# A hybrid decoder block on one Trainium2 core: output projection and expert queries of two chunks from one filling of the weights, stages dealt anew, residual summed by TensorE

## The chip, the cores and the metric

One core of a Trainium2 chip. The metric is the time of one execution on the device in microseconds, the median of three runs. All data are float32.

## The reference

One decoder layer over 1024 tokens of width 1024, in chunks of 128 tokens. Cut to what matters:

```python
h = _rmsnorm(x, ln1_w)
proj = h @ w_in                       # 3592 columns, split for retention and gated DeltaNet
y_r = ...                             # retention, 4 heads, state carried from chunk to chunk
y_g = ...                             # gated delta rule, 4 heads, a triangular solve per chunk
x = x + concat([y_r, y_g]) @ w_out
h2 = _rmsnorm(x, ln2_w)
q = h2 @ peer_wq                      # 8 heads x 2 halves x 128
s = q . peer_keys                     # top 16 of 128 per half, top 16 of 256 sums
act = gelu(peer_u[ids] . h2)          # 128 experts for each token
x = x + sum(softmax(best) * act * peer_v[ids])
y = _rmsnorm(x, lnf_w)
```

Each token picks 128 experts, and each expert's rows of `peer_u` and `peer_v` are fetched by an indirect transfer: 8 KB for a token and expert, over 1 GB for the whole input.

## The kernel before

The sequence is eight chunks n = 0 to 7 of 128 tokens. The program is written by hand for each engine, with semaphores; nothing is scheduled automatically.

**Expert steps.** A chunk has 64 steps, 512 in all, numbered through. A step takes two gathers of 1 MB (`uv<-uv_tab,ids`, L459 on GpSimd) into a ring of ten buffers `uv`. VectorE forms the dot product of the u half with the token (L1209), ScalarE makes the gelu (L886) and two scaled diagonals (L892), TensorE multiplies the v halves by them into two PSUM banks, one pair of banks for each chunk (L488, eight instructions a step), and that frees the two ring buffers (`v_used`, for which GpSimd waits). TensorE works one step behind. After a chunk's last step, `add_sums` on VectorE (L1220) adds the banks to `acc` (the chunk's rows after the output projection), ScalarE squares and takes the root (L902, L904), VectorE scales (L1228), ScalarE issues the store. These run in steps 3 and 4 of the next chunk.

**Everything else is dealt between the steps.** Every engine walks the same list of stages and asks before each piece for the steps up to a place (`Stream`, `chunks`):

- *mix n*: convolution, retention, delta rule with the inversion of a triangular matrix in seven levels, then output projection (`out0`, `out1`), the residual sum, the transposes of the second norm and the queries of heads 0 to 3 (`q0`, `q1`, scores `s0`). Its pieces lie at places given by the weights `PIECES`, one `turn()` each.
- *route n*: the queries `q2`, `q3` and scores, the copies of the normalised row for the dot products (`replicate`), on VectorE the top 16 searches and the indices of the experts, and then the input projections of the next chunk or pair (`inputs`). Chunks 2+3, 4+5, 6+7 ("first", "second") share one filling of the input weights: each weight block is multiplied by both chunks' columns, `actT` and `actT_ahead`.

Where a stage lies is set by `window(n)`: the stages end at steps -3 (mix 0), 22, 55, 83, 118, 138, 176, 206, 244, 264, 304, 334, 372, 392, 436 and 456 (route 7). Route n must have found the experts of chunk n before step 64 n needs them.

**Weights.** The SP queue loads blocks of 1 MB: 14 for the inputs, 4 for the output projection, 8 for the queries. After the first ones they alternate between two buffers `wbuf`; a load waits for the last product that read its buffer. SP takes its list strictly in order, so a load that waits holds back all behind it. L540 (`rows_product`) and L548 (`cols_product`) are half projections, 16 or 32 instructions; `project` makes one for each source and half.

**Buffers.** `acc[n % 2]` takes the rows of chunk n and keeps the residual until the chunk is done; the load of chunk n waits until chunk n-2 is stored. `rowbuf` and `actT_ahead` (as `x_ahead`) also take the rows of the next chunks for the first norm. Products rotate through six PSUM banks in a queue (`take`).

## Time and profile before

| | |
|---|---|
| median of three runs | 3092.14 us (3088.72 to 3095.03) |
| span of the profiled execution | 3087.4 us |
| moved by DMA | 1265.78 MB, mean 410 GB/s |
| TensorE busy | 2363.0 us (77%), mean granted clock 0.879 |
| VectorE busy | 2096.2 us (68%) |
| ScalarE busy | 1174.9 us (38%) |
| GpSimd busy | 1164.5 us (38%) |

The span runs from the first instruction to the last one; it is the only time that the page gives of the profiled execution, and the median of the runs is 4.7 us above it. A busy share is a mean over stages that have different limits. Transfers are not an engine of the program: their busy share and rate stand in rows of their own. Line numbers are those of the kernel printed above.

### The profile page before, as it was taken

Reading aid. Unit: us, or ns where it says so; the run is one execution under the profiler, and the core shown is the slowest. Engines: PE = TensorE matmul, PEld = TensorE weight load, DVE = VectorE, ACT = ScalarE, POOL = GpSimd, SP = SyncE. Lnnn points to the kernel's source line nnn. Section 1 sums busy time; section 2 is a strip of 40 time slices with the busy share of each in tenths; the row PEclk is TensorE's granted clock in tenths of the full one; section 3 lists DMA queues with packets and bytes.
Section 4 is the critical chain, followed back from the end, with each engine's and each line's share of the span. In section 5 each row is a group of like instructions: output and inputs, shape, how many; then the busy total and the mean of one; then the engine's idle time right before and its main releaser. Section 6 shows DMA issues by size and latency. Waiting matters only on the chain.

```text
span 3087.4 us, 36329 instructions
## 1 busy us (share of the span) xinstructions
PE 2363.0 (77%) x12368; PEld 1353.8 (44%) x12368; DVE 2096.2 (68%) x5609; ACT 1174.9 (38%) x3433; POOL 1164.5 (38%) x1030
## 2 busy tenths in 40 slices
PE   8877787997875788897876688799787568866555
PEld 7753355763541345663452245575345124521111
DVE  5476955768579854767649974666856986497554
ACT  2243443344434432445323533434443443233222
POOL 0132533335433443324334443334433354335442
PEclk9999999999997899998997788899899788976777
DMA  8399999999999999999999999999999999999997
GB/s 354 139 410 426 427 427 411 414 403 416 426 426 404 426 427 426 417 418 426 427 426 415 424 426 427 417 404 419 427 426 426 413 427 427 427 407 425 427 427 333
DMA packets 177737, 1265.78 MB, mean 410 GB/s; under 512 B 21520, under 2 KB 21776, under 8 KB 25104
## 3 DMA queue, kind: packets, MB, share of 16 engines
q0 software_dynamic: 147456, 1073.81, 83.2%
q1 hardware_dynamic: 28368, 183.72, 14.3%
q10 hardware_dynamic: 1728, 5.94, 0.5%
q8 instruction: 98, 1.61, 0.2%
q14 instruction: 87, 0.71, 0.1%
HBM read 1259.19 MB, written 4.19 MB: 409 GB/s over the span
## 4 chain that ended last, share of the span: by engine, by line
PE 36%; DMA 30%; DVE 21%; ACT 7%; issue 4%; POOL 2%; ACTq 0%; POOLq 0%; DVEq 0%
DMA uv<-uv_tab,ids 25%; PE bank L488 13%; DVE uv L1209 10%; PE bank L548 9%; PE bank L540 8%; DMA wbuf<-w 5%; PE bank L555 2%; ACT diag L892 2%; POOL uv L459 2%; DVE area L1519 1%; DVE area L1274 1%; DVE area L1515 1%; PE bank L515 1%; PE bank L570 1%; DVE arena L1575 1%
## 5 line engine op out<-in xcount | busy, mean ns | idle before, releaser
L459 POOL DMA_INDIRECT uv<-uv_tab,ids x1024 | 1164.0, 1137 | 1890.0 <-PE bank L488 1542.2
L1209 DVE CUSTOM_DVE_ANT_0 uv<-uv,h 128x1024 f32<-128x1024 f32 x1024 | 1238.5, 1224 | 733.4 <-DMA uv<-uv_tab,ids 722.2
L488 PE MATMUL bank<-uv,diag 128*64 128x512 f32 x4096 | 1197.2, 717 | 532.3 <-ACT diag L892 528.8
L488 PEld LDWEIGHTS bank<-uv,diag 128*64 128x64 f32 x4096 | 288.9, 155 | 1205.5 <-ACT diag L892 751.5
L886 ACT ACTIVATE gelu<-dots 128x2 f32<-128x2 f32 x512 | 104.1, 203 | 1334.0 <-DVE dots L1209 1313.6
L548 PE MATMUL bank<-actT,wbuf 128*128 128x128 f32 x2688 | 338.8, 287 | 34.7 <-DMA wbuf<-w 29.8
L548 PEld LDWEIGHTS bank<-actT,wbuf 128*128 128x128 f32 x2688 | 326.4, 202 | 83.9 <-issue 67.5
L892 ACT ACTIVATE diag<-gated,gelu 128x64 f32<-128x64 f32 x1024 | 300.6, 340 | 59.9 <-ACT gelu L886 2.0
L882 ACT ACTIVATE gated<-smalls,gate 128x64 f32<-128x64 f32 x1024 | 294.3, 336 | 15.2 <-DVE acc L1228 15.2
L540 PE MATMUL bank<-wbuf,actT 128*128 128x256 f32 x960 | 227.1, 390 | 17.2 <-DMA wbuf<-w 15.3
L540 PEld LDWEIGHTS bank<-wbuf,actT 128*128 128x128 f32 x960 | 181.6, 194 | 89.1 <-issue 50.4
L555 PEld LDWEIGHTS bank<-arena 128*128 128x128 f32 x1016 | 127.9, 201 | 63.1 <-issue 45.9
L555 PE MATMUL bank<-arena 128*128 128x128 f32 x1016 | 141.7, 293 | 4.6 <-DVE arena L1418 2.4
L886 ACT ACT_TABLE_LOAD x92 | 118.0, 1283 | 1.6
L1519 DVE FIND_INDEX8 area<-area,arena 128x8 uint32<-128x128 f32 (+1 forms) x384 | 100.4, 280 | 0.0
L540 PE MATMUL bank<-wbuf,actT_ahead 128*128 128x256 f32 x384 | 88.7, 384 | 0.0
L1515 DVE MAX8 area<-arena 128x8 f32<-128x128 f32 (+1 forms) x384 | 81.8, 275 | 6.3 <-ACT arena L1126 4.6
L1209 DVE DVE_READ_ACCUMULATOR2_ANT dots<- 128x1 f32 x1024 | 84.2, 82 | 0.0
L1274 DVE SCALAR_TENSOR_TENSOR area<-conv_in,conv_w,area 128x128 f32<-128x128 f32 x288 | 82.1, 347 | 2.5
L540 PEld LDWEIGHTS bank<-wbuf,actT_ahead 128*128 128x128 f32 x384 | 71.5, 190 | 23.6 <-issue 14.6
L605 PE MATMUL bank<-keys_sb,arena 128*128 128x128 f32 x256 | 43.1, 318 | 44.5 <-ACT arena L914 42.8
L914 ACT ACTIVATE conv_in<-bank 128x512 f32<-128x512 f32 x24 | 14.3, 598 | 149.9 <-PE bank L548 149.8
(226 smaller groups left out, 1910.7 us busy)
## 6 DMA issues: line engine op xcount, KB each, us to landing
wbuf<-w SPq DMA_DIRECT2D x146, 1024.0 KB
uv<-w SPq DMA_DIRECT2D x20, 1024.0 KB, 18.1
uv<-uv_tab,ids POOLq DMA_INDIRECT x1024
acc<-x SPq DMA_DIRECT2D x8, 512.0 KB
y<-acc ACTq DMA_DIRECT2D x8, 512.0 KB
rowbuf<-x SPq DMA_DIRECT2D x5, 512.0 KB, 12.8
actT_ahead<-x SPq DMA_DIRECT2D x3, 512.0 KB, 18.8
keys_sb<-keysT ACTq DMA_DIRECT2D x1, 1024.0 KB, 12.9
```

Source lines behind the costliest of these rows:

```text
L459: nc.gpsimd.indirect_dma_start(out=uv[i % RING][:, :, :].rearrange("p z d -> p (z d)"), out_offset=None, in_=uv_tab, in_offset=bass.Indire ...
L488: done = mm(sums[s // PAIRS][z][64 * j:64 * j + 64, :], diag[:, i % DIAGS, :], uv[i % RING][:, 1, 512 * z:512 * z + 512], start=(s % PAIRS ...
L540: last = mm(b[:, WB * half_:WB * half_ + WB], src[:, k, :], wb[:, k, :], start=(k == 0), stop=(k == KT - 1))
L548: last = mm(b[:, o:o + P], wb[:, k, P * i:P * i + P], src[:, k, :], start=(k == 0), stop=(k == KT - 1))
L555: last = mm(b[:, P * h:P * h + P], lhs[:, h, :], rhs[:, h, :], start=True, stop=True)
L882: made = A(gated[:, step % 2, j, :], stack, ACT.Copy, scale=gate[n % 2][:, j, pair:pair + 1])
L886: A(gelu[:, step % 2, :], dots[:, d0:d0 + 2], ACT.Gelu).then_inc(S["gelu"], 1)
L892: made = A(diag[:, (2 * step + j) % DIAGS, :], gated[:, step % 2, j, :], ACT.Copy, scale=gelu[:, step % 2, j:j + 1])
L1209: V.tensor_tensor_reduce(out=u, in0=u, in1=h2[n % 2][:, j, :], scale=1.0, scalar=0.0, op0=ALU.mult, op1=ALU.add, accum_out=dots[:, i % DOT ...
L1274: last = V.scalar_tensor_tensor(dst, src, conv_w[:, i, j:j + 1], dst, ALU.mult, ALU.add)
L1515: last = V.max(vals(t)[:, o:o + 8], src(t))
L1519: last = V.max_index(index(t)[:, o:o + 8], vals(t)[:, o:o + 8], src(t))
```

## The change

**One filling for two chunks.** Chunks 4+5 and 6+7 (`JOINT`) make output projection and queries together. Mix 4 now ends after the mixed columns' transposes. Mix 5 makes its own, then multiplies each block of `w_out` and `peer_wq` by both chunks' columns (`out_and_first_queries`, `next_joint_queries`), with `actT` for chunk 4 and `actT_ahead` for chunk 5. Heads 4 to 7 follow in route 4, for both chunks; route 5 has only the search. The same for 6 and 7. The queries and scores of two chunks at once lie in `qT`, `scores`, `vnew` and `kst` (half of `rowbuf`).

**Stages dealt anew.** The new list `STAGES` gives each stage's end: -3, 22, 52, 76, 106, 124, 155, 178, 203 (mix 4), 244 (mix 5), 264 (route 4), 286 (route 5), 317 (mix 6), 372 (mix 7), 392 (route 6), 414 (route 7). In mix 5 and 7 `PIECES` sums to 47.9 for 37.9; in mix 4 and 6 to 27.1.

**Residual by TensorE.** At a chunk's first step TensorE multiplies `acc` by the identity into the two sum banks, which start from that; `add_sums` is gone, and ScalarE squares and VectorE scales straight from the banks, in halves. The output is staged in the other `acc`, so the load of chunk n waits for the store of chunk n-3.

**Waits.** The load of `x_ahead` for chunk 7 waits for `rep3` of chunk 5 (the last reader of `actT_ahead`, at step 264), the load of chunk 6's rows into `rowbuf` for the scores `s3` of chunk 5. TensorE may take a later bank of its queue where the first would be freed too late (`HELD`), and the sum banks of a finished chunk return to the queue at step 6.

```diff
+JOINT = (4, 5, 6, 7)
+TOGETHER = ("x2", "qT", "scores")
+def key(n):
+    return KIND[n] + "'" * (n in JOINT)
...
+        for j in range(2):
+            uses += both_chunks(f"out{j}", "x2", 2, j)
+        uses += [(f"h2T{j}-", "h2T", 2, j, -1) for j in range(2)] + h2T
+        for i in range(4):
+            uses += both_chunks(f"q{i}", "qT", 4, i) + both_chunks(f"s{i}", "scores", 4, i)
+        return uses + [(f"rep{i}-", "rep", 4, i, -1) for i in range(4)] + rep
...
-PIECES = ([2, 2.3, 1.7, 1, 1.6, 1.2, 2, 1.5]
-          + [1.2, 0.8, 0.7, 0.8, 1.3, 0.8, 1.2, 0.8, 0.7, 0.8, 0.5, 0.8] + [0.6, 0.8, 1.4, 0.6]
-          + [1.15, 1.15, 1.15, 1.15] + [0.8, 0.8] + [1.15, 1.15, 1.15, 1.15])
-WINDOW = {"first": (16, 14), "second": (12, 8), None: (12, 8)}
-def window(n):
-    if n < 0:
-        return -1, -1
-    if n < 3:
-        return ((-3, 22), (55, 83), (118, 138))[n]
-    before, after = WINDOW[KIND[n + 1] if n + 1 < NCH else None]
-    return PAIRS * n - before, PAIRS * n + after
+MIXED = ([2, 2.3, 1.7, 1, 1.6, 1.2, 2, 1.5]
+         + [1.2, 0.8, 0.7, 0.8, 1.3, 0.8, 1.2, 0.8, 0.7, 0.8, 0.5, 0.8] + [0.6, 0.8, 1.4, 0.6])
+PIECES = {key(n): MIXED + [1.15] * 4 + [0.8, 0.8] + [1.15] * 4 for n in range(NCH)}
+PIECES["first'"] = MIXED
+PIECES["second'"] = MIXED + [1.15] * 8 + [0.8, 0.8, 0.8] + [1.15] * 8
+STAGES = [("route", -1, -1), ("mix", 0, -3), ("route", 0, 22), ("mix", 1, 52), ("route", 1, 76), ("mix", 2, 106),
+          ("route", 2, 124), ("mix", 3, 155), ("route", 3, 178), ("mix", 4, 203), ("mix", 5, 244), ("route", 4, 264),
+          ("route", 5, 286), ("mix", 6, 317), ("mix", 7, 372), ("route", 6, 392), ("route", 7, 414)]
...
+        def queries(n, j):
+            if n not in JOINT:
+                return qT[:, 4 * j:4 * j + 4, :]
+            if j == 3:
+                return kst if later_of_two(n) else vnew
+            o = (12, 8, 12)[j]
+            return scores_of_chunk(n)[:, o:o + 4, :]
+        def scores_of_chunk(n):
+            return qT if later_of_two(n) else scores
...
                 if c.kind == "first":
+                    if n - 1 in JOINT:
+                        sp.wait_ge(full, PLACE[n - 1, "rep3"] + 1)
                     sp.dma_start(x_ahead, x[n + 1]).then_inc(ahead_loaded, 16)
                 if c.kind != "second":
                     weights(range(2 if n == 0 else 0, IN_BLOCKS))
-                if n >= 2:
-                    sp.wait_ge(y_stored, 16 * (n - 1))
-                sp.dma_start(acc[n % 2][:, :], x[n]).then_inc(x2_loaded, 16)
-                weights(range(IN_BLOCKS, BLOCKS))
+                if n == 2:
+                    sp.wait_ge(x2_taken, 1)
+                if n >= 3:
+                    sp.wait_ge(y_stored[(n - 3) % 2], 32 * ((n - 3) // 2 + 1))
+                sp.dma_start(acc[n % 2][:, :], x[n]).then_inc(x2_loaded[n % 2], 16)
+                if key(n) != "first'":
+                    weights(range(IN_BLOCKS, BLOCKS))
                 if n + 1 < NCH and KIND[n + 1] != "second":
                     sp.wait_ge(*event("ss2", n))
+                    if n in JOINT:
+                        sp.wait_ge(full, PLACE[n, "s3"] + 1)
                     sp.dma_start(rowbuf[:, :], x[n + 1]).then_inc(x_loaded, 16)
...
-                    queue.extend((sums[-2][j], ("y_sum", s // PAIRS - 1, j)) for j in range(2))
-                if s == 0:
-                    pe.wait_ge(*event("x2", 0, 1))
+                if s % PAIRS == SUMS_FREE and s > PAIRS:
+                    queue.extend((sums[-2][j], ("y_out", s // PAIRS - 1, j)) for j in range(2))
+                if s % PAIRS == 0:
+                    n = s // PAIRS
+                    pe.wait_ge(*event("x2", n, 1))
+                    for z in range(2):
+                        taken = mm(sums[n][z][:, :], ident, acc[n % 2][:, 512 * z:512 * z + 512], start=True, stop=False,
+                                   skip_group_check=True)
+                    taken.then_inc(x2_taken, 1)
                 pe.wait_ge(diag_made, s + 1)
                 for z in range(2):
                     for j in range(2):
                         i = 2 * s + j
                         done = mm(sums[s // PAIRS][z][64 * j:64 * j + 64, :], diag[:, i % DIAGS, :],
-                                  uv[i % RING][:, 1, 512 * z:512 * z + 512], start=(s % PAIRS == 0),
+                                  uv[i % RING][:, 1, 512 * z:512 * z + 512], start=False,
                                   stop=(s % PAIRS == PAIRS - 1), skip_group_check=True)
...
+                at_ = next(i for i, (_, e) in enumerate(queue) if e is None or e[1] != n or name not in HELD.get(e[0], ()))
+                free, freed = queue.pop(at_)
...
+            def next_joint_queries(n, j, between):
+                banks, done = [take(n, f"s{j - 1}" + mark) for mark in ("-", "")], [0]
+                def then():
+                    between()
+                    done[0] += 1
+                    if done[0] <= 2:
+                        joint_scores(n - 2 + done[0], j - 1, banks[done[0] - 1])
+                project(n, f"q{j}", cols_product, [actT, actT_ahead], then, ("-", ""))
...
+            def out_and_first_queries(n, turn):
+                for j in range(2):
+                    project(n, f"out{j}", rows_product, [actT, actT_ahead], turn, ("-", ""))
+                turn()
+                for m, mark in ((n - 1, "-"), (n, "")):
+                    for j in range(2):
+                        pe.wait_ge(*event("x2", m, j))
+                        transposes(n, f"h2T{j}" + mark, lambda i: acc[m % 2][:, P * (4 * j + i):P * (4 * j + i) + P], 4)
+                    turn()
+                pe.wait_ge(*event("h2T", n, 1))
+                project(n, "q0", cols_product, [actT, actT_ahead], turn, ("-", ""))
+                next_joint_queries(n, 1, turn)
...
+                elif key(n) == "first'":
+                    steps = iter(range(1, 9))
+                    for j in (2, 3):
+                        next_joint_queries(n + 1, j, lambda: at(next(steps) / length(n)))
+                    at(9 / length(n))
+                    banks = [take(n + 1, "s3" + mark) for mark in ("-", "")]
+                    for a in range(2):
+                        joint_scores(n + a, 3, banks[a])
+                    replicate(n + 1, "-")
+                elif n in JOINT:
+                    replicate(n, "", actT_ahead)
...
-                act.wait_ge(*event("y_sum", n, 1))
-                A(h2[n % 2][:, 0, :], acc[n % 2][:, :], ACT.Square, accum_out=st[:, 60:61]).then_inc(S["yss"], 1)
-                act.wait_ge(*event("yss", n))
-                A(st[:, 59:60], st[:, 60:61], ACT.Sqrt, bias=eps_col[:, 0:1], scale=1.0 / D).then_inc(S["sqrt_y"], 1)
-                act.wait_ge(*event("y_out", n))
-                act.dma_start(out[n], acc[n % 2][:, :]).then_inc(y_stored, 16)
+                y = stage(n)
+                act.wait_ge(v_used, PAIRS * (n + 1))
+                if n + 1 < NCH:
+                    act.wait_ge(x2_taken, n + 2)
+                A(y[:, 0:512], sums[n][0][:, :], ACT.Square, accum_out=st[:, 58:59]).then_inc(S["yss"], 1)
+                A(y[:, 512:1024], sums[n][1][:, :], ACT.Square, accum_out=st[:, 60:61]).then_inc(S["yss"], 1)
+                act.wait_ge(*event("yss", n, 0))
+                A(st[:, 56:57], st[:, 58:59], ACT.Identity, bias=eps_col[:, 0:1], scale=1.0 / D).then_inc(S["yss"], 1)
+                act.wait_ge(*event("yss", n, 2))
+                A(st[:, 59:60], st[:, 60:61], ACT.Sqrt, bias=st[:, 56:57], scale=1.0 / D).then_inc(S["sqrt_y"], 1)
+                for j in range(2):
+                    act.wait_ge(*event("y_out", n, j))
+                    act.dma_start(out[n][:, 512 * j:512 * j + 512], y[:, 512 * j:512 * j + 512]).then_inc(y_stored[n % 2], 16)
...
+            def joint_sums(c, turn):
+                for j in range(2):
+                    for _ in range(4):
+                        turn()
+                    for m, mark in ((c.n - 1, "-"), (c.n, "")):
+                        x2 = acc[m % 2][:, 512 * j:512 * j + 512]
+                        dve.wait_ge(x2_loaded[m % 2], 16 * (m // 2) + 16)
+                        V.tensor_tensor(x2, filled(dve, f"out{j}" + mark, c)[:, :], x2, ALU.add).then_inc(S["x2"], 1)
+                for _ in range(5):
+                    turn()
+                second_factors(c.n - 1)
+                second_factors(c.n)
...
-                if step < STEPS and pair == FINISH and n > 0 and j == 1:
-                    add_sums(n - 1)
                 if step < STEPS and pair == FINISH + 1 and n > 0 and j == 1:
                     finish(n - 1)
-            def add_sums(n):
-                y = acc[n % 2]
-                dve.wait_ge(v_used, PAIRS * (n + 1))
-                for j in range(2):
-                    V.tensor_tensor(y[:, 512 * j:512 * j + 512], sums[n][j][:, :], y[:, 512 * j:512 * j + 512], ALU.add
-                                    ).then_inc(S["y_sum"], 1)
             def finish(n):
-                y = acc[n % 2]
+                y = stage(n)
                 dve.wait_ge(*event("sqrt_y", n))
                 V.reciprocal(st[:, 57:58], st[:, 59:60]).then_inc(peer_chain, 1)
                 dve.wait_ge(peer_chain, n + 1)
-                V.scalar_tensor_tensor(y[:, :], y[:, :], st[:, 57:58], lnf_row[:, :], ALU.mult, ALU.mult
-                                       ).then_inc(S["y_out"], 1)
+                for j in range(2):
+                    V.scalar_tensor_tensor(y[:, 512 * j:512 * j + 512], sums[n][j][:, :], st[:, 57:58],
+                                           lnf_row[:, 512 * j:512 * j + 512], ALU.mult, ALU.mult).then_inc(S["y_out"], 1)
```

How the order moves, on the SP queue, from the loads of chunk 4 on. Before:

```order
L429 DMA ropes<-rope 128x64
L431 DMA actT_ahead<-x 128x1024
L417 DMA wbuf<-w 128x2048 x14
L436 DMA acc<-x 128x1024
L417 DMA wbuf<-w 128x2048 x12
L429 DMA ropes<-rope 128x64
L436 DMA acc<-x 128x1024
L417 DMA wbuf<-w 128x2048 x12
L440 DMA rowbuf<-x 128x1024
L429 DMA ropes<-rope 128x64
```

Now:

```order
L499 DMA ropes<-rope 128x64
L503 DMA actT_ahead<-x 128x1024
L487 DMA wbuf<-w 128x2048 x14
L510 DMA acc<-x 128x1024
L499 DMA ropes<-rope 128x64
L510 DMA acc<-x 128x1024
L487 DMA wbuf<-w 128x2048 x12
L517 DMA rowbuf<-x 128x1024
```

The 12 blocks of chunk 4 for output and queries are gone, and those of chunk 5 serve both; the same holds for 6 and 7.

TensorE, mix 5: the queries of heads 0 to 3 (L548, now L632) between the steps' matmuls (L488, now L571); L605, now L695, are scores. Before:

```order
L548 MATMUL bank<-actT,wbuf 128x128 x16
L488 MATMUL bank<-uv,diag 64x512 x4
L548 MATMUL bank<-actT,wbuf 128x128 x16
L488 MATMUL bank<-uv,diag 64x512 x4
L548 MATMUL bank<-actT,wbuf 128x128 x16
L488 MATMUL bank<-uv,diag 64x512 x4
L605 MATMUL bank<-keys_sb,arena 128x128 x4
L548 MATMUL bank<-actT,wbuf 128x128 x16
L488 MATMUL bank<-uv,diag 64x512 x4
```

Now:

```order
L632 MATMUL bank<-actT,wbuf 128x128 x16
L571 MATMUL bank<-uv,diag 64x512 x4
L632 MATMUL bank<-actT_ahead,wbuf 128x128 x16
L571 MATMUL bank<-uv,diag 64x512 x4
L632 MATMUL bank<-actT,wbuf 128x128 x16
L571 MATMUL bank<-uv,diag 64x512 x4
L632 MATMUL bank<-actT_ahead,wbuf 128x128 x16
L571 MATMUL bank<-uv,diag 64x512 x4
L632 MATMUL bank<-actT,wbuf 128x128 x16
L571 MATMUL bank<-uv,diag 64x512 x4
L695 MATMUL bank<-keys_sb,arena 128x128 x4
```

Each half of a block's columns is now projected for `actT` and for `actT_ahead`, still with one step after each.

TensorE, the input projections of chunks 6 and 7 in route 5 (L540 and L548, now L624 and L632). Before:

```order
L548 MATMUL bank<-actT,wbuf 128x128 x16
L548 MATMUL bank<-actT_ahead,wbuf 128x128 x16
L488 MATMUL bank<-uv,diag 64x512 x4
L548 MATMUL bank<-actT,wbuf 128x128 x16
L488 MATMUL bank<-uv,diag 64x512 x4
L548 MATMUL bank<-actT_ahead,wbuf 128x128 x16
L548 MATMUL bank<-actT,wbuf 128x128 x16
L488 MATMUL bank<-uv,diag 64x512 x4
L548 MATMUL bank<-actT_ahead,wbuf 128x128 x16
L488 MATMUL bank<-uv,diag 64x512 x4
L548 MATMUL bank<-actT,wbuf 128x128 x16
```

Now:

```order
L632 MATMUL bank<-actT,wbuf 128x128 x16
L571 MATMUL bank<-uv,diag 64x512 x4
L632 MATMUL bank<-actT_ahead,wbuf 128x128 x16
L632 MATMUL bank<-actT,wbuf 128x128 x16
L571 MATMUL bank<-uv,diag 64x512 x4
L632 MATMUL bank<-actT_ahead,wbuf 128x128 x16
L632 MATMUL bank<-actT,wbuf 128x128 x16
L571 MATMUL bank<-uv,diag 64x512 x4
L632 MATMUL bank<-actT_ahead,wbuf 128x128 x16
L632 MATMUL bank<-actT,wbuf 128x128 x16
```

From the first to the seventh half projection lay four steps, now three: two half projections to each step.

## Rows read from the trace of the kernel before

**Rows 1.** The page: two engines, then DMA share and GB/s in 40 slices.

```profile
PE 2363.0 (77%) x12368; PEld 1353.8 (44%) x12368; DVE 2096.2 (68%) x5609; ACT 1174.9 (38%) x3433; POOL 1164.5 (38%) x1030
...
DMA  8399999999999999999999999999999999999997
GB/s 354 139 410 426 427 427 411 414 403 416 426 426 404 426 427 426 417 418 426 427 426 415 424 426 427 417 404 419 427 426 426 413 427 427 427 407 425 427 427 333
```

**Rows 2.** Windows by stage: mix 1, route 1, route 2, route 3, route 5, route 7, tail.

```profile
core 0: us, PE busy (x) PEld busy (x) DVE busy (x) ACT busy (x) POOL busy (x), PEclk, DMA share, GB/s
297.00:475.00 178.00, 136.16 (x727) 78.39 (x724) 126.61 (x289) 79.81 (x229) 72.90 (x64) 0.91 1.01 427
475.00:666.00 191.00, 172.65 (x1069) 123.09 (x1068) 126.26 (x398) 67.96 (x195) 61.74 (x53) 0.96 0.99 408
...
871.00:986.00 115.00, 71.38 (x340) 31.21 (x338) 105.90 (x364) 42.39 (x121) 44.88 (x40) 0.78 0.99 411
...
1193.00:1384.00 191.00, 171.80 (x1045) 122.91 (x1042) 130.90 (x406) 74.71 (x214) 60.79 (x56) 0.95 1.01 419
...
1929.00:2125.00 196.00, 176.35 (x1080) 125.91 (x1081) 130.61 (x406) 74.63 (x214) 68.42 (x58) 0.96 1.01 412
...
2693.00:2808.00 115.00, 74.60 (x336) 31.96 (x336) 105.97 (x364) 42.87 (x123) 45.21 (x39) 0.77 0.99 412
2808.00:3073.00 265.00, 156.69 (x444) 34.51 (x440) 136.30 (x223) 69.68 (x275) 117.58 (x104) 0.74 1.00 421
```

**Rows 3.** The page: SP's queue and the weight blocks.

```profile
q1 hardware_dynamic: 28368, 183.72, 14.3%
...
wbuf<-w SPq DMA_DIRECT2D x146, 1024.0 KB
```

**Rows 4.** Windows over the input stretches of routes 1, 3 and 5, columns as above.

```profile
535.00:675.00 140.00, 140.00 (x819) 102.05 (x816) 98.02 (x301) 49.09 (x146) 48.47 (x41) 0.98 1.00 409
1253.00:1393.00 140.00, 140.00 (x820) 101.59 (x816) 97.11 (x293) 49.70 (x144) 45.38 (x42) 1.00 1.01 417
1989.00:2129.00 140.00, 138.78 (x818) 101.12 (x818) 96.60 (x293) 52.07 (x153) 49.74 (x42) 0.99 1.00 406
```

**Rows 5.** The same window of route 3, the steps' matmuls (L488) alone: PE, PEld.

```profile
1253.00:1393.00 140.00, 39.35 (x164) 9.70 (x160) 1.00 1.01 417
```

**Rows 6.** Order of time, TensorE in route 3: start us, us, engine, line.

```profile
1320.41 3.72 PE L540 MATMUL bank<-wbuf,actT 128*128 128x256 f32 x16
1324.07 1.94 PE L488 MATMUL bank<-uv,diag 128*64 128x512 f32 x8
1325.93 3.72 PE L540 MATMUL bank<-wbuf,actT_ahead 128*128 128x256 f32 x16
```

**Rows 7.** Groups of instructions: VectorE's dot product and its read-out.

```profile
L1209 DVE CUSTOM_DVE_ANT_0 uv<-uv,h 128x1024 f32<-128x1024 f32 x1024 | 1238.5, 1224 | 733.4 <-DMA uv<-uv_tab,ids 722.2 <-issue 4.4 <-DVE area L1515 0.4
...
L1209 DVE DVE_READ_ACCUMULATOR2_ANT dots<- 128x1 f32 x1024 | 84.2, 82 | 0.0
```

**Rows 8.** Windows: early mix 1, early mix 3, late route 2, columns as in rows 2.

```profile
297.00:397.00 100.00, 70.14 (x363) 34.65 (x359) 91.12 (x219) 49.26 (x130) 46.10 (x40) 0.89 1.01 426
986.00:1106.00 120.00, 85.17 (x412) 39.65 (x410) 101.45 (x237) 54.28 (x149) 52.84 (x47) 0.82 1.01 426
904.00:984.00 80.00, 44.57 (x172) 12.46 (x170) 78.02 (x265) 31.16 (x89) 34.74 (x31) 0.76 0.99 404
```

**Rows 9.** VectorE's longest wait in mix 1, then in mix 3: us, times, longest.

```profile
DVE uv L1209 <- DMA uv<-uv_tab,ids: 29.9, 18, 3.1
...
DVE uv L1209 <- DMA uv<-uv_tab,ids: 43.7, 27, 3.4
```

**Rows 10.** The page and the groups: x ahead, 128x512 matmul, additions of the sums.

```profile
actT_ahead<-x SPq DMA_DIRECT2D x3, 512.0 KB, 18.8
...
L560 PE MATMUL bank<-arena,tab 128*128 128x512 f32 x32 | 19.6, 697 | 14.3 <-DVE arena L1318 14.3
...
L1220 DVE TENSOR_TENSOR acc<-bank,acc 128x512 f32<-128x512 f32 x16 | 10.3, 685 | 4.7 <-PE bank L488 4.7
```

215 lines of the change are left out of this document (164 added, 51 removed).

## The prediction

> **What bounds the kernel now.** I read the page first. The transfers are busy in almost every slice, at 426 or 427 GB/s where nothing disturbs them, while no engine is busy for more than 77% of the span [rows 1]. So the floor is bytes over rate: 1265.78 MB at 427 GB/s are 2964 us of the 3087.4 us span. The 123 us above that are lost rate, and the view of stages [rows 2] says where. The kernel runs 512 expert steps, each with two gathers of 1 MB, and everything else is dealt between them; the windows are cut at the steps where the program changes from a mixer ("mix n") to a routing stage ("route n"), found by counting VectorE's dot products. A step costs 2 x 1.049 MB / 0.427 = 4.91 us of transfers. In the pure tail 56 steps took 265 us; I use 4.9.
>
> Two kinds of stage fall below 427. First, the stages in which two chunks are projected (route 1, 3, 5: 408, 419, 412 GB/s). Inside each lies a stretch of about 140 us in which TensorE is busy without a gap [rows 4]. The order of time confirms it: a half projection starts, 3.66 us later a step's eight matmuls, 1.86 us after those the next half projection [rows 6], and the granted clock is 1.00 of 2.4 GHz [rows 4]. Second, the routing stages without projections (route 2, 7: 411, 412 GB/s), where VectorE is busy 78.0 of 80 us and the rate is down to 404 [rows 8]. Mixers run at 427 or close to it.
>
> **The sum**, against the profiled span of 3087.4 us. The median of the runs lies 4.7 us above it, and I carry that difference over.
>
> *1. The weights.* The order shows 24 blocks fewer on the SP queue: 166 become 142. A block is 1024 KB [rows 3], 2.46 us at 427 GB/s, so **-59 us** while transfers set the pace. The blocks leave mix 4, route 5, mix 6 and route 7. The same sum by the Trainium skill, "DMA: Bandwidth & Descriptors", section Where 436 GB/s comes from: the port ceiling of 435 GB/s would make it -58, its HBM share of about 358 GB/s would make it -70; the trace's 427 is well above the latter and decides.
>
> *2. The input stretches.* Both chunks of a pair must now be mixed before the routing of the first, so the stages ahead shrink. From the transposes of the second chunk to the last input product the order counts 20, 22 and 22 steps before, 17, 17 and 16 now. The products stay. In such a stretch TensorE ends last: its steps cost 39.35 us for 164 of 8 matmuls each, 20.5 steps, so 1.92 us a step [rows 5]. A step taken out gives back 1.92 us there, and costs 4.9 us where it is put, in the tail, where the transfers end last. 14 steps x 3.0 us = +42 us. Against that, the ring holds ten 1 MB buffers and part of it is in flight when TensorE falls behind; I credit one buffer of 2.46 us for each stretch: **+35 us**. Bounds: 0, if TensorE has room I don't see; +42, if nothing is absorbed.
>
> *3. Routing stages paced by VectorE.* A step is 2 x (1.224 + 0.082) = 2.61 us of VectorE [rows 7]. Route 2 loses 2 of its 20 steps and gives back about 2.7 to 4.9 us each: +3. Route 7 gains 2 steps and loses four blocks: VectorE needs 106.0 + 5.2 = 111.2 us, at its best share of 78.0/80 that is 114, against 115 before [rows 2, 8], so of the blocks' 9.8 us and the steps' 9.8 us nothing is left over and a little may be lost: +3. **+6 us**, between 0 and 10.
>
> *4. The joint queries* (routes 4 and 6) put eight half projections into the first eight of 20 steps: TensorE 3.66 + 1.86 = 5.5 us and the scores now and then, transfers 4.9 + 1.2 = 6.1. A tie. But the last scores now come at step 9.3 of 20 where they came at 5.3, and VectorE wants them at step 10 with the following dot products queued behind: 2 us each, **+4 us**, between 0 and 10 (a whole step each).
>
> *5. Denser mixers.* Mix 1, 2, 3 go from 33, 35, 38 steps to 30, 30, 31; mix 5 does 1.26 times the listed work in 41 steps instead of 40. In the first 100 us of mix 1 VectorE is busy for 91.1 us [rows 8]; in the new deal that part has 1.8 steps less, so 86.4 us of work against 92 of transfers: still hidden, barely. Local gaps: **+4 us**, between 0 and 34 (below).
>
> *6. A new wait.* The load of chunk 7's rows stands behind the copy of chunk 5's normalised columns (step 264), and lands about 19 us after [rows 10], while ScalarE wants it from step 267: a wait of one step, with the diagonals of that step queued behind it, and behind those TensorE and the gathers. In flight are several gathers of 2.46 us; **+2 us**, between 0 and 9. Behind it on SP stand 14 weight blocks, needed from step 271; they arrive in time.
>
> *7. The residual.* VectorE loses 16 additions of 0.685 us, TensorE gains 16 matmuls of 128x512, each two instructions, by the nearest row 19.6 us for 32 of them, so 2.4 us for a chunk [rows 10]. Where VectorE paces (three chunk ends) this gives 3 x 1.4 = 4; one pair lands inside an input stretch, +2; the end of the kernel loses two additions and gains a second square: -1. **-3 us**, between -6 and +5.
>
> Sum: -59 + 35 + 6 + 4 + 4 + 2 - 3 = **-11**, a span of 3076 and a time of about **3081 us**.
>
> A step dealt into the tail costs little else: there the granted clock is 0.74, so TensorE is between its 1.2 and 2.4 GHz levels, and busy 156.7 us in 56 steps, 2.8 us a step [rows 2], well under 4.9.
>
> **The rivals.**
>
> *A. TensorE has room in the input stretches.* Term 2 is then 0: 3081 - 35 = **3046 us**. For it: its weight loads are busy only 101.6 of 140 us [rows 4], and the rate in these stretches is still 406 to 417 GB/s. Against it: the starts follow each other without a gap [rows 6], and the rate is already below 427. The Trainium skill, "Perfetto Trace Analysis", section Identifying the Most-Contended Engine, sides with this rival: matmul busy time says little of how near TensorE is to its limit, and the weight loads' busy share is the better measure. By that rule 27% would be free. I hold that the start-to-start spacing is the stronger witness, since the program's order leaves nothing to fill such room with. Chance 0.17.
>
> *B. Slower: VectorE paces the compressed mixers.* Place: mix 1, 2 and 3, which lose 3, 5 and 7 steps. If VectorE and its round trips to TensorE, not transfers, end last there, a removed step gives back 2.61 instead of 4.9 us: 15 x 2.3 = 34 us instead of the 4 counted, **3111 us**. It decides once VectorE's wait for gathers there is gone: 29.9 us in mix 1 and 43.7 in mix 3 [rows 9], of which the new deal needs 7 and 16. For it: VectorE is busy 91.1 of 100 and 101.5 of 120 us in the early parts [rows 8]. Against: waits remain by that count. Chance 0.16.
>
> *C. The new waits eat the rest.* Term 4 at 10, its upper bound, and term 6 at 9 give 3081 + 6 + 7 = **3094 us**, no change that can be told. For it: both waits sit in front of dot products or diagonals, on engines that take their work in order. Against: each is covered by several gathers in flight. Chance 0.15.
>
> That the change does not do what it says is ruled out by the order: 24 loads are gone.
>
> **How the numbers follow.** The forecast has 0.52. A measurement of this kernel can tell about 0.2%, 6 us: under 3086 is faster, over 3098 slower. The forecast's own range, 3065 to 3097, lies to about 0.7 below 3086, most of the rest in the band. Faster: 0.37 + 0.17 of A + 0.03 of B and C where they come out small = 0.57. Slower: B, and the upper ends of C and of the forecast, 0.20. Same: 0.23. The range reaches to A and most of the way to B: 3046 to 3106 us.
>
> **What would show it.** Queue q1 down from 183.72 MB by 25.2 MB, with the total near 1240.6 MB. Mix 4 and mix 6 about 63 + 20 and 34 + 20 us shorter than before, at 427 GB/s. The input stretches 127 to 135 us long, TensorE without a gap, and the rate down to 340 to 375 GB/s (two half projections and one step are 3.15 MB in 7.3 + 1.9 us): this is term 2, and if the rate there stays above 400 it is wrong and A is right. Mix 1 to 3 at 420 GB/s or more; below 400, with VectorE no longer waiting for gathers, B is right. Route 4 and 6 within 3 us of their 117. The tail, 98 steps, near 4.9 us a step. A long wait of ScalarE for the rows of chunk 7 near step 267 would show term 6. The prediction is wrong if the rate in mixers falls, or if the transfers are not the last to end in the tail.

## The result: slower by 1.9%

| | before | after |
|---|---|---|
| median | 3091.78 us (4 runs, 3088.72 to 3095.03) | 3150.78 us (4 runs, 3147.30 to 3152.25) |
| ratio | | 1.0188, 95% interval 1.0176 to 1.0201 |
| span of the profiled execution | 3087.4 us | 3145.5 us |
| moved by DMA | 1265.78 MB | 1240.62 MB |
| TensorE clock granted, mean | 0.879 | 0.879 |

The page of the kernel after: rate in 40 slices, total, and the two large queues.

```profile
GB/s 356 143 414 420 413 420 371 355 375 420 419 419 336 419 419 366 338 408 420 419 419 419 419 372 346 392 419 408 419 420 419 419 418 407 420 420 420 420 420 327
DMA packets 175434, 1240.62 MB, mean 394 GB/s; under 512 B 21264, under 2 KB 21520, under 8 KB 25872
...
q0 software_dynamic: 147456, 1073.81, 83.6%
q1 hardware_dynamic: 24912, 158.55, 12.5%
```

The bytes went as forecast: q1 has 158.55 MB where it had 183.72 [rows 3], 25.17 less. But the best slices now read 419 to 420 GB/s, where they read 426 or 427 [rows 1]. That is one surprise. The other stands in the stages. Windows of the kernel after by stage: mix 1, route 1, mix 2, mix 3, route 3, mix 4, route 4, route 5.

```profile
core 0: us, PE busy (x) PEld busy (x) DVE busy (x) ACT busy (x) POOL busy (x), PEclk, DMA share, GB/s
299.00:466.00 167.00, 131.86 (x714) 75.05 (x710) 119.03 (x279) 77.07 (x217) 71.50 (x60) 0.91 1.01 417
466.00:655.00 189.00, 169.51 (x1018) 126.20 (x1019) 115.53 (x383) 63.38 (x174) 46.47 (x44) 0.92 0.94 365
655.00:834.00 179.00, 146.66 (x782) 86.36 (x781) 118.55 (x274) 82.72 (x229) 77.81 (x64) 0.94 1.00 408
947.00:1128.00 181.00, 138.93 (x699) 76.81 (x696) 125.92 (x295) 80.84 (x226) 67.47 (x61) 0.88 0.94 383
1128.00:1307.00 179.00, 165.11 (x1037) 124.33 (x1036) 111.17 (x372) 60.60 (x169) 46.50 (x44) 0.94 0.97 375
1307.00:1453.00 146.00, 112.90 (x561) 59.52 (x562) 107.20 (x255) 72.21 (x188) 67.57 (x54) 0.90 0.97 395
1676.00:1792.00 116.00, 88.96 (x604) 53.81 (x604) 105.82 (x365) 49.62 (x140) 47.07 (x41) 0.93 1.01 419
1792.00:1949.00 157.00, 135.80 (x773) 95.89 (x774) 108.57 (x368) 52.47 (x151) 41.68 (x40) 0.92 0.94 368
```

Routes 1, 3 and 5 are down to 365, 375 and 368 GB/s (408, 419, 412 before [rows 2]), and mix 3 and mix 4 to 383 and 395.

One measure serves for everything below. The **lost time** of a stage is its length times (1 - rate/427), with the rate of its window: what it takes beyond moving its bytes at 427 GB/s. Rates are whole numbers, so a stage is known to about 0.5 us.

### The profile page after: what moved, and what is told of

Same layout as the page of the kernel before. It is cut to its first block, busy times and chain, and to the rows that moved or that the text cites. A ratio compares the mean times of both kernels' runs of the same rounds, so it can differ in the third digit from the quotient of the medians.

```text
span 3145.5 us, 36400 instructions
## 1 busy us (share of the span) xinstructions
PE 2379.8 (76%) x12400; PEld 1351.0 (43%) x12400; DVE 2089.7 (66%) x5601; ACT 1175.2 (37%) x3454; POOL 1156.2 (37%) x1030
## 2 busy tenths in 40 slices
DMA packets 175434, 1240.62 MB, mean 394 GB/s; under 512 B 21264, under 2 KB 21520, under 8 KB 25872
## 3 DMA queue, kind: packets, MB, share of 16 engines
q0 software_dynamic: 147456, 1073.81, 83.6%
q1 hardware_dynamic: 24912, 158.55, 12.5%
## 4 chain that ended last, share of the span: by engine, by line
PE 35%; DMA 32%; DVE 21%; ACT 6%; issue 4%; POOL 2%; ACTq 0%; POOLq 0%; DVEq 0%
DMA uv<-uv_tab,ids 26%; PE bank L571 12%; DVE uv L1408 9%; PE bank L632 9%; PE bank L624 7%; DMA wbuf<-w 6%; POOL uv L536 2%; PE bank L639 2%; ACT diag L1024 1%; DVE area L1491 1%; DVE area L1736 1%; DVE area L1732 1%; PE bank L654 1%; PE bank L599 1%; PE bank L745 1%
## 5 line engine op out<-in xcount | busy, mean ns | idle before, releaser
L1408 DVE CUSTOM_DVE_ANT_0 uv<-uv,h 128x1024 f32<-128x1024 f32 x1024 | 1239.5, 1224 | 723.2 <-DMA uv<-uv_tab,ids 715.6
L571 PE MATMUL bank<-uv,diag 128*64 128x512 f32 x4096 | 1205.7, 721 | 576.4 <-ACT diag L1024 576.2
L571 PEld LDWEIGHTS bank<-uv,diag 128*64 128x64 f32 x4096 | 289.0, 156 | 1278.2 <-ACT diag L1024 842.5
L632 PE MATMUL bank<-actT,wbuf 128*128 128x128 f32 x2176 | 270.8, 285 | 29.0 <-DMA wbuf<-w 23.9
L632 PEld LDWEIGHTS bank<-actT,wbuf 128*128 128x128 f32 x2176 | 260.6, 200 | 64.4 <-issue 52.9
L624 PE MATMUL bank<-wbuf,actT 128*128 128x256 f32 x832 | 196.8, 391 | 14.7 <-DMA wbuf<-w 14.5
L624 PEld LDWEIGHTS bank<-wbuf,actT 128*128 128x128 f32 x832 | 158.2, 194 | 69.3 <-issue 37.1
L632 PEld LDWEIGHTS bank<-actT_ahead,wbuf 128*128 128x128 f32 x1088 | 124.3, 192 | 17.0 <-issue 17.0
L632 PE MATMUL bank<-actT_ahead,wbuf 128*128 128x128 f32 x1088 | 129.3, 277 | 0.0
L624 PE MATMUL bank<-wbuf,actT_ahead 128*128 128x256 f32 x512 | 118.6, 385 | 0.0
L624 PEld LDWEIGHTS bank<-wbuf,actT_ahead 128*128 128x128 f32 x512 | 95.0, 190 | 34.5 <-issue 22.7
L1736 DVE FIND_INDEX8 area<-area,arena 128x8 uint32<-128x128 f32 (+1 forms) x320 | 84.2, 282 | 0.0
```

The lines of the kernel that those rows point to most:

```text
L571: done = mm(sums[s // PAIRS][z][64 * j:64 * j + 64, :], diag[:, i % DIAGS, :], uv[i % RING][:, 1, 512 * z:512 * z + 512], start=False, sto ...
L624: last = mm(b[:, WB * half_:WB * half_ + WB], src[:, k, :], wb[:, k, :], start=(k == 0), stop=(k == KT - 1))
L632: last = mm(b[:, o:o + P], wb[:, k, P * i:P * i + P], src[:, k, :], start=(k == 0), stop=(k == KT - 1))
L1408: V.tensor_tensor_reduce(out=u, in0=u, in1=h2[n % 2][:, j, :], scale=1.0, scalar=0.0, op0=ALU.mult, op1=ALU.add, accum_out=dots[:, i % DOT ...
L1736: last = V.max_index(index(t)[:, o:o + 8], vals(t)[:, o:o + 8], src(t))
```

## Experiments 1: eight words in a small buffer

The diff of `build` has a line that neither the change's description nor the prediction gave weight: the buffer `st` grew from 92 to 100 words, and everything allocated behind it, the ten gather buffers `uv` first of all, starts 32 bytes later. In the program's allocation the gather buffers began at byte 124416 of a partition, a multiple of 512, and now begin at 124448. Such a shift alone was put into the kernel before, with `st` of 100 words as here, or of 108, 124 and 156.

```diff
-        st = sb("st", [92])
+        st = sb("st", [100])
```

**b_shift32.**

> Kernel before with one edit: the small buffer st has 100 words instead of 92, as the change has it, so that everything allocated behind it, the ten gather buffers uv among them, starts 32 bytes later. Theory address (the gather buffers' start, no longer a multiple of 512 bytes, costs DMA rate): the stretches that ran at 426 to 427 GB/s run at 419 to 420, and the time is about 3092 + 50 = 3142 us. Rival (the fall from 427 to 420 GB/s came from the change's own transfers or from its order of work): 426 to 427 GB/s and 3092 us, within 5.

**b_shift64.**

> Kernel before with st of 108 words: everything behind it starts 64 bytes later. Theory address in the form 'a multiple of 64 bytes is enough': 427 GB/s and 3092 us. In the form '512 bytes, or 128, are needed': 419 to 420 GB/s and about 3142 us. Rival (address has no part): 3092 us.

**b_shift128.**

> Kernel before with st of 124 words: everything behind it, the gather buffers among them, starts 128 bytes later. If a multiple of 128 bytes is enough: 427 GB/s and 3093 us. If 256 is needed: 420 to 421 GB/s and about 3130 us, as with 64.

**b_shift256.**

> Kernel before with st of 156 words: everything behind it, the gather buffers among them, starts 256 bytes later, at a multiple of 256 and not of 512. If a multiple of 256 bytes is enough: 427 GB/s and 3092 us, within 5. If 512 is needed: about 420 GB/s and 3130 to 3140 us, as with shifts of 32 and 64 bytes.

**b_behind32**, with `sb("pad", [8])` on the line behind `uv` and `st` as it was.

> Kernel before with a pad of 8 words behind the gather buffers: h2, ids, gate, dots and what follows start 32 bytes later, the gather buffers stay at their multiple of 512 bytes. If it is the gather buffers' own address that costs: 427 GB/s and 3091 us, within 5. If the tables of indices or what VectorE and ScalarE read behind them take part: between 3100 and 3136.

| kernel before, with | median | ratio to before, 95% |
|---|---|---|
| everything behind `st` moved by 32 bytes | 3136.17 us | 1.0143 (1.0125 to 1.0160) |
| by 64 | 3129.79 us | 1.0123 (1.0106 to 1.0140) |
| by 128 | 3125.38 us | 1.0105 (1.0090 to 1.0121) |
| by 256 | 3093.57 us | 0.9998 (0.9989 to 1.0007) |
| only what lies behind the gather buffers, by 32 | 3093.00 us | 1.0001 (0.9991 to 1.0010) |

The page's rate line of four of them, in this order: moved by 32, by 128, by 256, and only what lies behind.

```profile
GB/s 345 142 401 420 420 419 402 410 403 414 420 419 406 420 420 419 412 417 420 419 420 400 420 419 419 409 412 418 419 420 408 405 420 419 420 397 420 420 420 327
```

```profile
GB/s 346 144 410 421 421 408 413 413 397 421 421 420 408 421 421 420 385 415 420 421 421 415 420 421 421 408 410 420 421 421 404 414 421 421 421 400 421 421 421 321
```

```profile
GB/s 354 141 412 426 427 427 392 416 399 419 427 426 406 427 427 425 411 415 423 427 426 415 425 426 427 417 405 421 427 426 426 407 427 427 426 404 425 427 427 335
```

```profile
GB/s 348 144 401 426 427 426 406 408 401 418 426 426 408 427 427 426 411 418 418 427 426 422 422 426 427 421 403 417 426 426 426 411 427 427 426 409 424 427 427 333
```

The best slices tell it: 419 to 420, 420 to 421, then 426 to 427 again in both. Between `st` and the gather buffers lie only `bn`, `mv` and `iota_f`, which no transfer writes, and VectorE's dot product takes the same 1223 or 1224 ns. So it is where the gathers write, and of the starts tried those at a multiple of 256 bytes cost nothing. The cost is 1.4, 1.2 and 1.1% of the time for 32, 64 and 128 bytes; neighbours among these overlap in their intervals, and only the first and the last are just apart. The Trainium skill, "DMA: Bandwidth & Descriptors", section How a descriptor splits into AXI transactions, names this boundary: of reads it says that a descriptor which doesn't start at a multiple of 256 bytes begins with a transaction from the boundary below, whose unused bytes still cost beats. With that boundary the runs agree, here on the written side. The beats don't give the sizes. By the Trainium skill's figures, as an estimate, a gathered row of 8 KB would take 1, 2 and 4 beats more on 256 for the three shifts, 0.4, 0.8 and 1.6%, and the runs show about the same loss for all three, if anything the other way round.

This is shown for the gathers, whose queue carries 1073.81 of the 1240.62 MB. The weight buffers, `acc` and `rowbuf` start 64 bytes above a multiple of 256 in every kernel here, the one before included (`wbuf` at byte 26176). Whether that costs anything no run tests.

**a_aligned**, the kernel after with `st` of 220 words.

> Kernel after with st of 220 words, so that the gather buffers start at a multiple of 512 bytes again, as they did before the change; nothing else is changed. Theory address: 426 to 427 GB/s where 419 to 420 were, 3151 - 52 = about 3099 us, within 8, so that the rest of the change costs about 7 us. Rival (the rate fell through the work itself): 3151 us and 420 GB/s.

Measured: 3104.42 us, ratio 1.0043 (1.0029 to 1.0057), span 3103.1 us. So **46 us** of the 59 are this address; in the kernel before the same line costs 44. But without it the change is still slower by 12 us, where the forecast had it 11 faster. Its windows: route 1, mix 2, mix 3, route 3, mix 4, route 5, mix 6, tail.

```profile
460.00:647.00 187.00, 170.11 (x1038) 126.69 (x1037) 115.42 (x383) 64.54 (x177) 47.61 (x44) 0.93 0.94 372
647.00:825.00 178.00, 148.25 (x785) 87.42 (x784) 118.62 (x277) 82.59 (x229) 77.00 (x64) 0.93 1.00 413
937.00:1115.00 178.00, 135.42 (x705) 75.02 (x702) 125.30 (x291) 81.63 (x227) 67.17 (x62) 0.90 0.94 386
1115.00:1294.00 179.00, 163.28 (x1032) 123.20 (x1031) 111.78 (x376) 60.27 (x170) 45.51 (x43) 0.95 0.96 376
1294.00:1440.00 146.00, 111.32 (x560) 58.78 (x559) 106.73 (x250) 71.94 (x187) 65.81 (x54) 0.92 0.97 397
1774.00:1928.00 154.00, 137.29 (x780) 96.56 (x777) 108.33 (x369) 53.50 (x155) 42.54 (x40) 0.92 0.95 373
1928.00:2094.00 166.00, 124.48 (x592) 62.14 (x592) 120.23 (x271) 74.70 (x208) 76.64 (x64) 0.89 0.98 404
2618.00:3093.00 475.00, 279.79 (x782) 62.13 (x780) 242.01 (x395) 127.24 (x494) 214.08 (x188) 0.74 1.00 423
```

The lost time by stage in us, from such windows of each kernel (three of the experiments below are in the same table):

```
              before  a_aligned  a_half_inputs  a_deal  a_thin3
start to 22     68.4       66.5           69.3    73.1     67.7
mix 1            0.0        1.9            2.3     2.7      2.3
route 1          8.5       24.1            7.7    19.6     24.4
mix 2            3.3        5.8            1.2    11.9      5.4
route 2          4.3        0.3            0.3     1.9      0.3
mix 3            0.0       17.1           18.2    16.9     10.7
route 3          3.6       21.4            3.1    11.4     22.0
mix 4            0.5       10.3            1.0    10.3      9.9
mix 5            0.0        0.5            2.6     2.1      1.0
route 4          2.7        0.5            0.3     0.3      0.3
route 5          6.9       19.5            9.0    20.1     23.5
mix 6            0.5        8.9            2.3     8.2      9.3
mix 7            0.0        2.1            3.5     3.3      3.5
routes 6, 7      6.5        5.2            6.0     0.7      4.7
tail             5.0        4.4            4.5     8.1      4.4
sum            110.3      188.6          131.1   190.4    189.6
```

25.16 MB less at 427 GB/s are 58.9 us won; 78.3 us more are lost. That makes +19 us against the 15.7 by which the spans differ, and the rounding of the rates covers the rest. Each column is one profiled execution, and these can lie off their run's median (a_deal 3107.2 us against 3102.6). In the first row, where the five kernels do nearly the same work, they differ by up to 6.6 us, so a few us in one stage mean little. The loss has two parts: the input stretches in routes 1, 3 and 5, 19.0 us before and 65.0 now, and the mixers, 4.3 before and 46.6 now. All kernels named a_ below have the gather buffers aligned and are to be read against a_aligned.

## Experiments 2: the input stretches

```diff
-                        last = product(b, half_, wb, src)
+                        last = product(b, half_, wb, src, KT // 2 if n >= 2 and name in IN_NAMES else KT)
```

**a_half_inputs** leaves out half of TensorE's work in the input projections of chunks 2 to 7: 4 of the 8 pieces of the inner dimension. The products take the number of pieces as their last argument.

> Kernel after, gather buffers aligned (st of 220 words), with half of TensorE's work in the input projections of chunks 2 to 7 left out (4 of the 8 pieces of the inner dimension; the weights are still loaded, all steps and all stages stay). Theory PE (TensorE paces the input stretches, and its backlog at their end is what mixes 2, 4 and 6 lose in their first 30 us): routes 1, 3 and 5 go from 372 to 376 GB/s to at least 415, which is about 50 us, and mixes 2, 4 and 6 win some 15 more: 3104 - 65 = about 3040 us. If only the input stretches are TensorE's, and the mixers' loss has another cause: 3104 - 50 = 3054. Rival (the gathers and weights themselves, or VectorE's choosing, pace these stretches): 3095 to 3104.

Measured: 3046.17 us, ratio 0.9853 (0.9838 to 0.9868), 58 us below a_aligned. Windows over the stretches of routes 1, 3 and 5 in a_aligned:

```profile
528.00:658.00 130.00, 128.21 (x739) 95.89 (x739) 78.68 (x247) 39.90 (x110) 33.40 (x31) 0.97 0.92 349
1180.00:1310.00 130.00, 128.93 (x765) 98.32 (x766) 79.18 (x251) 36.39 (x99) 32.69 (x31) 1.00 0.93 349
1820.00:1945.00 125.00, 124.54 (x734) 95.39 (x733) 76.26 (x244) 34.95 (x93) 28.54 (x28) 1.00 0.91 348
```

and in a_half_inputs, then its mixes 2, 3, 4 and 6:

```profile
528.00:658.00 130.00, 101.15 (x500) 59.52 (x496) 91.52 (x292) 51.98 (x133) 46.44 (x40) 0.93 0.97 404
1180.00:1310.00 130.00, 100.00 (x466) 55.33 (x466) 97.09 (x302) 64.02 (x154) 46.91 (x44) 0.92 1.01 426
1800.00:1925.00 125.00, 93.12 (x398) 50.51 (x394) 83.56 (x248) 57.08 (x139) 44.64 (x40) 0.89 0.96 392
638.00:806.00 168.00, 131.49 (x693) 73.31 (x690) 119.25 (x277) 76.22 (x215) 70.12 (x60) 0.90 1.01 424
919.00:1096.00 177.00, 133.26 (x680) 73.54 (x676) 125.48 (x292) 80.83 (x226) 67.50 (x60) 0.88 0.93 383
1260.00:1397.00 137.00, 99.70 (x508) 50.74 (x510) 106.26 (x251) 66.26 (x178) 68.19 (x54) 0.90 1.01 424
1872.00:2033.00 161.00, 115.64 (x556) 55.08 (x558) 120.87 (x272) 74.78 (x207) 71.95 (x64) 0.90 1.00 421
```

In the upper rows PE is busy 381.7 of 385 us and the rate is 349, 349 and 348 GB/s. With half of the work left out it is busy 294 us, and the rate is 404, 426 and 392. Routes 1, 3 and 5 lose 20 us instead of 65, at 408, 419 and 400 GB/s, of which only route 3 reaches the 415 expected; and mixes 2, 4 and 6, in which nothing was changed, lose 4.5 instead of 25. So **TensorE paces the input stretches, and its backlog at their end is what the next mixer loses**: at the start of mix 4 in a_aligned ScalarE, which makes the diagonals and copies the gates in one order, stands 7.2 and then 4.9 us for the last half projections. Mix 3 has no input stretch ahead and stays at 18.

**a_deal** puts steps back there:

```diff
-STAGES = [("route", -1, -1), ("mix", 0, -3), ("route", 0, 22), ("mix", 1, 52), ("route", 1, 76), ("mix", 2, 106),
-          ("route", 2, 124), ("mix", 3, 155), ("route", 3, 178), ("mix", 4, 203), ("mix", 5, 244), ("route", 4, 264),
-          ("route", 5, 286), ("mix", 6, 317), ("mix", 7, 372), ("route", 6, 392), ("route", 7, 414)]
+STAGES = [("route", -1, -1), ("mix", 0, -3), ("route", 0, 22), ("mix", 1, 52), ("route", 1, 78), ("mix", 2, 106),
+          ("route", 2, 128), ("mix", 3, 155), ("route", 3, 180), ("mix", 4, 203), ("mix", 5, 244), ("route", 4, 264),
+          ("route", 5, 290), ("mix", 6, 320), ("mix", 7, 372), ("route", 6, 392), ("route", 7, 424)]
```

> Kernel after, gather buffers aligned (st of 220 words), stages dealt otherwise: the input stretches, which are routes 1, 3 and 5, get 26, 25 and 26 steps instead of 24, 23 and 22; route 2 ends at step 128, so that the sum banks of chunk 2 are taken between two stages and not inside mix 3; the steps come from mixes 2, 3, 4, 6 and 7 (28, 27, 23, 30, 52) and from the tail (88 steps instead of 98). Theory of the prediction, term 2 (TensorE paces the input stretches, a step put back there is worth 3.0 us) with the bank wait gone too: 8 x 3.0 + 9 = 33 us less than 3104, so 3071 us, below the kernel before. Rival (the mixers, made denser again, lose what the input stretches win, through waits at their start): 3095 to 3110 us.

Measured: 3102.60 us (3093.20 to 3112.27), ratio 1.0021 (1.0009 to 1.0033). Windows: route 1, mix 2, mix 3, route 3, route 5.

```profile
470.00:660.00 190.00, 170.84 (x1044) 124.55 (x1045) 120.17 (x389) 67.56 (x192) 53.19 (x48) 0.94 0.97 383
660.00:829.00 169.00, 137.51 (x693) 81.21 (x694) 114.09 (x267) 75.01 (x207) 66.24 (x57) 0.90 0.98 397
963.00:1123.00 160.00, 122.93 (x624) 70.08 (x625) 112.71 (x264) 73.15 (x204) 57.16 (x52) 0.88 0.92 382
1123.00:1304.00 181.00, 171.70 (x1092) 127.35 (x1091) 116.83 (x384) 62.65 (x175) 51.32 (x48) 0.97 0.99 400
1775.00:1950.00 175.00, 153.25 (x818) 104.77 (x815) 118.69 (x386) 59.50 (x176) 54.34 (x47) 0.89 0.95 378
```

Route 3 wins 10 us of loss for two steps and route 1 4.5, but mix 2 loses 6 more, and route 5 wins nothing for its four, which the runs don't explain. The time lies in the range of the rival, that the loss moves.

**a_pieces** gives the first eight pieces of a mixer more steps, and the part with weights fewer. The first eight pieces of mixes 0, 5 and 7, which its expectation doesn't name, come from the same list and change too:

```diff
-MIXED = ([2, 2.3, 1.7, 1, 1.6, 1.2, 2, 1.5]
+MIXED = ([2.4, 2.8, 2.1, 1.2, 1.9, 1.5, 2.4, 1.8]
-PIECES = {key(n): MIXED + [1.15] * 4 + [0.8, 0.8] + [1.15] * 4 for n in range(NCH)}
+PIECES = {key(n): MIXED + [0.85] * 4 + [0.6, 0.6] + [0.85] * 4 for n in range(NCH)}
```

> Kernel after, gather buffers aligned (st of 220 words), stages as in after, but inside the mixers of chunks 1, 2 and 3 and the first mixers of the joint pairs the steps are dealt otherwise: the first eight pieces get 1.2 times their share, the pieces with output projection and queries 0.74 times. Theory VectorE (a mixer that is shortened loses at its start, where VectorE is 96% busy and then stands in turn with ScalarE; the part with weights has room): mix 3's lost time falls from 17 us to about 8, and the whole from 3104 to about 3095. Rival (the loss moves from the start to the part with weights): 3104, within 3.

Measured: 3121.74 us, ratio 1.0090 (1.0075 to 1.0106), 17 us worse: mix 3 lost 17.0 us as before, and route 1 27.9, mix 2 9.6, route 2 4.8. A miss for both theories.

**a_best** has the pieces of a_pieces, and mix 1 to mix 4 (with routes 1 to 3 between them) end at steps 51, 77, 106, 128, 156, 181 and 203.

> Kernel after, gather buffers aligned, pieces dealt as in the run a_pieces, and stages dealt so that routes 1 and 3 get 26 and 25 steps, route 2 22 and ends at step 128, mixes 1 to 4 get 29, 29, 28 and 22; the rest as in after. If each loss is paid where the theories put it (TensorE in routes 1 and 3: 14 us won back, as a_deal showed for those two; mix 3's start: 9 us): 3104 - 20 = about 3084 us, below the kernel before. Rival (the time lost per pair of chunks is fixed and only moves): 3100 us or more.

Measured: 3107.80 us, ratio 1.0054 (1.0041 to 1.0068): the rival's figure.

## Experiments 3: mix 3

Mix 3 had 38 steps and lost nothing; with 31 it loses 17 us, all in its first 60. But the steps alone don't set the loss: a_deal gave it 27, and it lost 16.9. In the kernel after, the first step of chunk 2 (step 128) and the end of chunk 1 fall inside it. Windows of 10 us from the start of mix 3, in a_aligned and then in the kernel before (it starts at 986 there):

```profile
936.00:946.00 10.00, 2.68 (x10) 0.52 (x6) 9.58 (x35) 5.71 (x12) 1.88 (x2) 0.67 1.02 425
946.00:956.00 10.00, 6.48 (x16) 1.67 (x16) 9.76 (x32) 5.26 (x12) 3.78 (x4) 0.67 0.70 267
956.00:966.00 10.00, 9.57 (x38) 4.45 (x39) 9.82 (x30) 7.20 (x17) 1.93 (x2) 0.70 0.99 390
966.00:976.00 10.00, 2.84 (x14) 2.02 (x14) 7.17 (x27) 9.77 (x18) 1.87 (x2) 0.81 0.78 296
976.00:986.00 10.00, 7.81 (x25) 2.27 (x25) 6.32 (x11) 5.18 (x16) 1.87 (x2) 0.85 0.36 120
986.00:996.00 10.00, 7.49 (x29) 2.25 (x26) 9.86 (x20) 4.28 (x13) 7.88 (x6) 0.84 0.92 334
```

```profile
986.00:996.00 10.00, 2.86 (x10) 0.76 (x8) 9.79 (x29) 6.64 (x16) 1.88 (x2) 0.67 1.01 428
996.00:1006.00 10.00, 5.06 (x20) 1.16 (x18) 9.32 (x30) 5.20 (x12) 6.59 (x6) 0.84 1.01 424
1006.00:1016.00 10.00, 8.51 (x36) 3.73 (x36) 9.86 (x28) 6.75 (x16) 1.98 (x3) 0.75 1.02 430
1016.00:1026.00 10.00, 6.75 (x30) 2.63 (x30) 7.36 (x26) 8.47 (x19) 6.66 (x6) 0.93 1.01 426
```

VectorE is busy 9.6 to 9.8 of 10 us in a_aligned at first and 9.3 to 9.9 before; but where the transfers run at 424 to 430 GB/s before, they fall to 267, 296 and 120. Waits in a_aligned from 972 to 1000 us (engine, what waited for what: us in all, times, longest):

```profile
POOL uv L536 <- PE bank L571: 16.7, 4, 12.5
...
PE bank L564 <- issue: 7.2, 1, 7.2
...
ACT gated L1014 <- DVE acc L1419: 5.2, 1, 5.2
```

TensorE stands 7.2 us before the residual's matmul. The profile names no releaser there, but it starts at 974.5 us, 0.1 us behind the end of ScalarE's late copy of a sum bank; ScalarE stands 5.2 us for VectorE's scaled output, with the diagonals behind it. Each was taken away.

```diff
-                        free, freed = queue.pop(0)
+                        at_ = next(i for i, (_, e) in enumerate(queue) if s != 2 * PAIRS or e[0] in ("gc_in", "norm_in"))
+                        free, freed = queue.pop(at_)
```

**a_bank128.**

> Kernel after, gather buffers aligned (st of 220 words), and one wait of TensorE taken away: at the first step of chunk 2 (step 128, in the middle of mix 3) the two sum banks are those released by gc_in and norm_in of chunk 3, not those of gc_in and E, which ScalarE had not yet copied. Theory bank (the 7.2 us for which TensorE stands there, with 102 to 346 GB/s beside it from 972 to 996 us, is lost time): 3104 - 9 = about 3095 us, and no stretch below 340 GB/s between 972 and 996 us. Rival (TensorE's wait only moves to the next thing late, for instance to ScalarE's diagonals): 3104 us, within 3.

Measured: 3106.81 us, ratio 1.0036 (1.0024 to 1.0048); mix 3 lost 14.7. TensorE's wait at the residual fell from 7.2 to 3.1 us, and that for the diagonals rose from 13.8 to 16.0 (from 940 to 1000 us in both). The time is the rival's.

With `STORE = 3`, and `store` waiting for `y_out` and issuing the stores:

```diff
+                if step % PAIRS == FINISH + STORE and step > FINISH + STORE:
+                    store(step // PAIRS - 1)
```

**a_store.**

> Kernel after, gather buffers aligned (st of 220 words); ScalarE issues the stores of a finished chunk's output, which wait for VectorE's y_out, three steps later than it computes the root, so that the diagonals of the steps between are no longer queued behind that wait (4.5 us at 983.9 to 988.4 us in a_aligned, inside mix 3). Theory store wait: mix 3's lost time falls from 17 us to about 9, and the other chunk ends lose 1 us less each: 3104 - 10 = about 3094 us. Rival (VectorE is behind there anyway, and the diagonals then wait for its dots): 3104, within 3.

**a_store_bank.**

> a_store and the other banks of a_bank128 together. If mix 3's loss is these two waits, one behind the other, so that taking one away alone only uncovers the other: mix 3 under 4 us lost, and 3104 - 15 = about 3089 us, below the kernel before. If its loss is VectorE's work at a mixer's start itself: 3100 us or more.

**b_store.**

> Kernel before with the same later store of a chunk's output (ScalarE's wait for y_out three steps later); st of 92 words. ScalarE stands 15 us in all there for VectorE's scaled output, but in routing stages, which lose only 3 to 4 us each at the chunk's end: 3092 - 5 = 3087 if the wait sets the pace there, 3092 if VectorE does.

**a_best2.**

> a_store_bank with route 3 given 25 steps and mix 4 23 (a_deal: route 3 lost 11 us instead of 21 with them, mix 4 no more than before). If the gains add up: 3089 - 10 = about 3079 us, below the kernel before. If they don't: 3100.

| | median | ratio, 95% | mix 3 lost |
|---|---|---|---|
| a_store | 3114.18 us | 1.0080 (1.0067 to 1.0093) | 17.4 us |
| a_store_bank | 3111.95 us | 1.0068 (1.0056 to 1.0080) | 15.6 us |
| b_store | 3091.97 us | 1.0003 (0.9994 to 1.0011) | 0.5 us |
| a_best2 | 3099.45 us | 1.0036 (1.0023 to 1.0049) | 15.3 us |

Neither wait is the cause of the 17 us, nor are both together, and in the kernel before the later store changes nothing. a_store even takes 10 us more than a_aligned, which the runs don't explain. The steps given back to route 3 pay again (12.2 us lost there instead of 18.3 in a_store_bank, 12.5 us less in all), but the whole is at the 3100 us of gains that don't add up.

**a_finish20** moves the whole end of chunk 1 from step 131 to step 148 (`FINISH` and `SUMS_FREE` 17 larger for that chunk).

> Kernel after, gather buffers aligned (st of 220 words); the end of chunk 1 (ScalarE's squares and root, VectorE's scaling, the store, the release of its two banks) comes 17 steps later, at step 148 instead of 131, behind the first half of mix 3. Theory chunk end (that work beside the mixer's start is what mix 3 loses by): its lost time falls from 17 us to under 6, 3104 - 11 = about 3093 us. Rival (VectorE's mixing work is enough by itself): mix 3 loses 14 us or more, and 3101 to 3106 us, or more if the two banks that are held longer are missed.

**a_thin3** leaves out two of the four taps of chunk 3's convolution: `for j in range(2 if n == 3 else 4)`.

> Kernel after, gather buffers aligned; of the short convolution of chunk 3 only two of the four taps are computed, which leaves out 24 of VectorE's instructions of 0.29 us, 7 us, in the first 35 us of mix 3. Theory VectorE (mix 3's start is paced by VectorE, 96 to 98% busy): about 7 of the 17 us lost there come back, 3097 us. Rival (the chunk's end is the cause, with its chain over ScalarE and TensorE's banks): under 2 us, 3102 to 3106.

Measured: a_finish20 3112.66 us, ratio 1.0067 (1.0055 to 1.0079), mix 3 lost 18.4 us; so ScalarE's and VectorE's work at the chunk's end isn't it. a_thin3 3106.30 us, ratio 1.0042 (1.0030 to 1.0054). Mix 3 in a_thin3, and of it the fifth and sixth 10 us:

```profile
938.00:1109.00 171.00, 132.19 (x686) 73.42 (x684) 119.52 (x270) 80.74 (x226) 72.42 (x60) 0.90 0.97 400
976.00:986.00 10.00, 7.80 (x30) 2.46 (x28) 8.37 (x15) 4.70 (x11) 4.60 (x5) 0.83 0.75 250
986.00:996.00 10.00, 6.52 (x36) 2.75 (x32) 9.90 (x21) 3.48 (x14) 8.17 (x7) 1.00 1.02 417
```

171 us instead of 178, and 10.7 us lost instead of 17.1, where every other kernel with the gather buffers aligned lost 14.7 to 18.4: with 7 us of VectorE's work left out, 6.4 us of loss are gone, most of it in the two windows shown (250 and 417 GB/s, where a_aligned has 120 and 334). So **VectorE's mixing work is part of what mix 3's start loses by**. That is one stage of one profiled execution. The whole does not show it: its time is the rival's, and routes 3 and 5 lost 4.6 us more, why isn't shown.

What takes the other 10.7 us stays open. VectorE isn't full where the rate is lowest. The windows with 296 and 120 GB/s hold 10.3 of the 17.1 us lost, and in them it is busy 7.17 and 6.32 us; it waits there 2.7 us for ScalarE and 2.8 us for TensorE. ScalarE is busy for 9.77 of 10 us in the first of them, with four table loads of 1.28 us that start there, where the window as far into the mixer had 8.47 before, at 426 GB/s. Its work is a rival that no run takes away. Why mix 1, as dense, loses only 2 us stays open too.

## Experiment 4: the residual

**b_residual**, the kernel before with the `+` lines of the residual (`x2_taken`, `start=False`, `SUMS_FREE`, `finish`) and nothing else.

> Kernel before with only the change's way of adding the residual: two identity matmuls of 128x512 at a chunk's first step put the residual into the sum banks, VectorE's two adds are gone, ScalarE squares the banks in two pieces, VectorE scales them in two pieces out of the banks, the banks come free at step 6 of the next chunk. st and all addresses are as before. Theory of the prediction: -3 us, so 3089 (bounds 3086 to 3097). Rival (the later release of the two banks, or TensorE's wait for the residual, makes routing stages longer): over 3097 us.

Measured: 3093.65 us, ratio 0.9997 (0.9988 to 1.0006): no change that can be told. The interval is -4 to +2 us and so holds the forecast's -3 as well; the rival, over 3097 us, is out.

## The prediction, step by step

It was wrong, in sign and by 70 us. The **decisive step is one that it didn't have**: no term for where the buffers start. The line `st = sb("st", [100])` costs 46 us, more than any error in the terms that were there. It stood in the edit, and the prediction left it out without a reason.

Without that the sum would have said 3081, where 3104 came. Its terms, in its own numbering, against a_aligned:

| term | forecast | measured | |
|---|---|---|---|
| 1 weights | -59 | -58.9 | 25.16 MB; right, as long as 427 GB/s is kept |
| 2 input stretches | +35 (0 to 42) | +46 | 65.0 less 19.0 us lost; mechanism right, size above its upper bound; rival A (room on TensorE, 3046 us) refuted |
| 3 routes 2 and 7 | +6 | -3 | 4.7 us lost in both, 8.1 before |
| 4 joint queries, routes 4 and 6 | +4 | -4 | 1.3 us lost, 5.4 before |
| 5 denser mixers | +4 (0 to 34) | +42 | 46.6 less 4.3 us lost; above its upper bound |
| 6 wait for chunk 7's rows | +2 | 0 | below |
| 7 residual | -3 (-6 to +5) | -1 (-4 to +2) | b_residual; can't be told from 0 or from -3 |

**Term 2** credited one gather buffer, 2.46 us, for each stretch. The loss came out above even the 42 us without that credit, so nothing of it shows, and the backlog went on behind the stretch. The named signs held in the kernel after: TensorE without a gap over about 130 us, and 343 to 353 GB/s there, inside the 340 to 375 named.

**Term 5 failed.** It weighed VectorE's work against the transfers over the first 100 us of mix 1 and called it "still hidden, barely" (its 92 us of transfers are 91 by its own 4.9 us a step). Two things were missed. A mixer behind an input stretch begins with TensorE late, so mixes 2, 4 and 6 lose 25 us that are really term 2's (a_half_inputs gives 20.5 of them back). And the start of mix 3 was not looked at in pieces of 10 us, where VectorE was already busy for 93 to 99%; a mean over 120 us hid that. The waits for gathers on which rival B was weighed, 29.9 us in mix 1 and 43.7 in mix 3, were read over whole mixers too. In the first 60 us of mix 3 there was next to none to give, in the kernel before:

```profile
DVE uv L1209 <- DMA uv<-uv_tab,ids: 0.9, 3, 0.4
```

In mix 1 it was 1.1 us. In a_aligned VectorE waits for no gather in the first 60 us of mix 3, though 36.4 us of such waits are left behind them. This half is in part rival B's mechanism (VectorE paces the compressed mixers), but in one mixer, where 17 us were lost and a_thin3 shows VectorE's hand in 6.4, against its price of 34 us.

**Term 6.** The instructions of line 1076, the squares of the rows, in the kernel after (min/median/max ns, then first and last start):

```profile
L1076 ACT ACTIVATE actT<-rowbuf x5: 1039/1056/1074, 4.1 to 1813.6; 128x1024 f32<-128x1024 f32 x5
...
L1076 ACT ACTIVATE actT<-actT_ahead x3: 1056/1056/1057, 514.6 to 1814.8; 128x1024 f32<-128x1024 f32 x3
```

The square of the rows loaded ahead starts at 1814.8 us, right behind that of the other rows at 1813.6, as in the kernel before: the load was in time.

**The tail** was right once aligned: 98 steps in 475 us, 4.85 each. **Mix 4** came out at 146 us where "63 + 20 us shorter" meant 132, and **mix 6** at 166 where 162 was meant; they lost 10 and 9 us, nearly all of which goes when the input work is halved (1.0 and 2.3 us left). **Rival C** (the new waits) is refuted by terms 4 and 6. The Trainium skill, "Perfetto Trace Analysis", section Identifying the Most-Contended Engine, sided with rival A: the weight loads' busy share is to show TensorE's limit better than matmul busy time. The trace doesn't agree here: in the stretches of a_aligned the weight loads are busy for 290 of 385 us, 75%, which would leave room, and there was none; the spacing of the starts was the better witness. And "the prediction is wrong if the rate in mixers falls" named the right sign.

No version here beats the kernel before; the best, a_best2 and a_deal, stay 0.2 to 0.4% above it.

## What to carry to other kernels

Where transfers set the pace, read a diff for addresses first: a new word ahead of the buffers that the gathers fill moved them all, and the rate of an undisturbed slice on the page showed it at once. A saving in bytes is worth its size only while nothing else becomes the last to end; making stages denser to reach it cost here where TensorE, and in part where VectorE, was already full, and a backlog was paid in the stage behind it. So sum up lost rate by stage, before and after, rather than busy shares.

## What was not expected of the hardware

Gathers into SBUF buffers moved by 32, 64 or 128 bytes off a multiple of 256 ran at 419 to 421 GB/s instead of 426 to 427, and the kernel took 1.4, 1.2 and 1.1% longer; moved by 256 bytes they ran as before. That the cost doesn't grow with the shift, and what in the write it is, these runs don't explain.
